# Attention of a diffusion trunk: transposes in three PSUM banks used from both ends, probabilities normalised on GpSimd before them, the sink as a score column

## The chip, the cores and the metric
One core of a Trainium2 chip runs the whole kernel. The metric is the device time of one execution in microseconds, as the median of several runs. The clock that the throttle grants to TensorE is given by the profile as a share of full speed (1.0 is 2.4 GHz, 0.5 is 1.2 GHz).
One core of a Trainium2 chip runs the whole kernel. The metric is the device time of one execution in microseconds, as the median of several runs. The clock that the throttle grants to TensorE is given by the profile as a share of full speed (1.0 is 2.4 GHz, 0.5 is 1.2 GHz).

## What is computed
Two layers of a trunk over 512 latent tokens and 256 context tokens with 1024 features. A layer has a gated feed-forward block (hidden width 2816), a mixer and a second feed-forward block; each starts with an RMS norm with a shift and scale from a conditioning vector. The mixer is the part that matters:

```python
u = modulate(rms_norm(h), shift, scale) @ w_in      # A: 6 query, 2 key, 2 value heads; B: the same; C: 256 channels
A: rotated q, k; each latent query block of 128 reads its own and the two neighbouring key blocks
   (|key - query| <= 128), all 256 context keys and a sink logit:
   p = softmax(concat([q k^T / 8 (masked), q k_ctx^T / 8, sink]))[without the sink]
B: normalised, rotated q, k; each latent query reads all 512 latent and 256 context keys, no sink
C: real part of a 2-D Fourier transform over positions and 64 channels, then a 64x64 map per group
h = h + gate * concat([A, B, C]) @ w_out
```

Context tokens go through the same layer and read only context keys (in A with the sink). In the last layer only the latent tokens' output is needed. Everything is float32.

## The kernel before
The features lie on the 128 partitions, the tokens along the free dimension: `h`, `xh`, `xl` are [128, 8, 768]. A float32 product is made in three passes of a rounded type (fp32r): each factor is split into a high part (`whi`, `xh`, a rounding copy on ScalarE) and a low part (`wlo`, `xl`, the difference, on VectorE), and TensorE adds hi x hi, hi x lo and lo x hi. Weights are streamed: SP loads the tile `raw` (two slots), ScalarE makes `whi` (L602), VectorE makes `wlo` (L938), TensorE multiplies into one of two accumulators `ring` (L1319). Each engine has its own queue in program order; waits are written out by hand as semaphore counts. There is no planner.

The mixer has three parts. First, 12 tiles of `w_in` (`act_w_in`, `dve_w_in`), with head norms and rotation on ScalarE, VectorE and GpSimd; queries and keys go to memory and come back stacked in `k2`, `q2`. After tile j = 1 TensorE makes the combined channel matrix (L1213) from `wf`, a small weight that SP has just loaded, and ScalarE copies it out at j = 2.

Second, the attention. The work is cut into score tiles (branch, key/value head, query block, head of the group), 72 in layer 0 and 48 in layer 1; three consecutive tiles share a query block and are called a trio here. With its context keys a query block has 4 or 5 key blocks of 128 in branch A, 6 in branch B, and 2 if it is a context block (layer 0 only). All engines run the same loop over i, and step i holds different stages of different tiles:

- TensorE: scores of tile i into `ring[i % 2]` (L1242 to L1247); transposes of the probabilities of tile i - LAG into `side` (L1261), a tile of two PSUM banks; and, in three of every three steps, a share of the value products of a finished trio into `bank[0]` (L1280). Before the first share it multiplies a matrix of ones with three diagonal matrices (L1276) into `bank[1]`: that spreads the reciprocal row sums over the partitions.
- VectorE: row maximum of tile i (L887) and a small operation that scales it, and in A takes the larger of it and the sink (L894, L896); the reciprocal of the row sum of tile i - 1 (L910), in A after adding the sink's exponential (L905); the low part `ptl` of the transposed tile i - LAG (L918); for a finished trio the sum of the two output parts (L929) and its product with the spread reciprocals (L931).
- ScalarE: the high part `pth` of the transposed tile (L719), a part of the trio's output (`corr`, L727), the exponential of tile i with its row sum (L737), in A the sink's exponential (L742), and the rounding of the trio's output into `xh` (L750).
- GpSimd: the diagonal matrix ident x reciprocal of each tile, 128 columns (L511), and the output's low part into `xl` (L498).

LAG is 2 and `prob` has P_RING = 3 buffers. The transposes of a tile wait until VectorE has made `ptl` of the tile before:

```python
pe.wait_ge(exp_done, si + 1)
if i >= 1:
    pe.wait_ge(pt_ready, si)
for m in range(nb):
    last = pe.transpose(side[:, m * P:(m + 1) * P], prob[:, i % P_RING, ...], ident[:])
```

At step 2 the loops make the Fourier part (TensorE L1180 and L1193), which uses `side` and both banks. Third, after the loop, 8 tiles of `w_out`: the first waits for the trios' outputs at its later k steps. The split of tile 12 (the first of `w_out`) is made during `w_in`; that of tile 13 (the second) when the first is multiplied. For each output tile VectorE adds the residual (L1044), ScalarE squares it for the next norm (L620), and ScalarE's and VectorE's queues have the split of the next weight tile behind that.

Of the kernel before, what the change touches and what calls it, by code (L numbers as in the profile page):

```python
# [15 lines left out]
F32 = mybir.dt.float32  # L16
# [6 lines left out]
P = 128  # L23
# [22 lines left out]
P_RING, LAG = 3, 2  # L46
# [85 lines left out]

def key_blocks(branch, q):

    if q >= 4:
        return []
    return list(range(max(0, q - 1), min(3, q + 1) + 1)) if branch == 0 else [0, 1, 2, 3]


def build(nc, x_t, ctx_t, c_cols, w_ada, b_ada, gains, g_final, qk_gain, sink, w_in, w_four, w_out,  # L140
# [4 lines left out]
    with ctx:  # L145
# [35 lines left out]
        sinks8 = sb("sinks8", [P, DEPTH * 6])  # L181
# [6 lines left out]
        row_max = sb("row_max", [P, 2])  # L188
        neg_max = sb("neg_max", [P, 4])
        row_sum = sb("row_sum", [P, 4])  # L190
        sink_exp = sb("sink_exp", [P, 4])
        row_tot = sb("row_tot", [P, 2])
# [43 lines left out]
        diag = sb("diag", [P, 2, 3, P], F32, work + 52224)  # L236
# [9 lines left out]
        side = ctx.enter_context(nc.psum_tensor("side", [P, 1024], F32))  # L246
        bank = [ctx.enter_context(nc.psum_tensor(f"bank{i}", [P, 512], F32)) for i in range(2)]
# [7 lines left out]
        cond_ready, sink_ready = sem("cond_ready"), sem("sink_ready")  # L255
# [24 lines left out]
        sc_done, max_done, nm_ready, exp_done = sem("sc_done"), sem("max_done"), sem("nm_ready"), sem("exp_done")  # L280
        tot_done, inv_ready, diag_done = sem("tot_done"), sem("inv_ready"), sem("diag_done")
        sink_exp_done = sem("sink_exp_done")
        p_turned, pth_done, pt_ready, pv_done = sem("p_turned"), sem("pth_done"), sem("pt_ready"), sem("pv_done")
        oadd_done = sem("oadd_done")
# [137 lines left out]
        def _(pool):  # L422
# [49 lines left out]
            for s in stages:  # L472
                layer, n, ow = s["layer"], s["n"], s["out_width"]
                if s["kind"] == "mix":
# [13 lines left out]
                    def rest_out(k):  # L488

                        b, kv, q, g = s["tiles"][3 * k]  # L490
                        tr = s["scores"] // 3 + k
                        here, cols = slice(kv * HD, kv * HD + HD), slice(q * P, (q + 1) * P)
                        pool.wait_ge(ohi_done, tr + 1)

                        pool.wait_ge(diag_done, s["scores"] + min(3 * k + 9, len(s["tiles"])))
                        if k >= 1:
                            pool.wait_ge(olo_done, tr)
                        pool.tensor_tensor(xl[here, 3 * b:3 * b + 3, cols], osum[here, k % 2].rearrange("p (g q) -> p g q", q=P),  # L498
                                           xh[here, 3 * b:3 * b + 3, cols].bitcast(F32), ALU.subtract).then_inc(olo_done, 1)

                    for i, (b, kv, q, g) in enumerate(s["tiles"]):
                        si = s["scores"] + i
                        if i == 0:
                            pool.wait_ge(f1_done, 6 * (layer + 1))
                        if g == 0 and i >= 9:
                            rest_out(i // 3 - 3)
                            pool.wait_ge(olo_done, si // 3 - 2)
# [1054 lines left out]
```

## Time and profile before
| | before |
|---|---|
| runs | 2894.14, 2893.08, 2893.99 us, median 2893.99 |
| profiled execution | 2893.89 us, its span 2892.1 us |
| busy: TensorE, VectorE, ScalarE, GpSimd | 2749.7 (95%), 1503.0 (52%), 1015.9 (35%), 676.7 (23%) us |
| mean granted clock | 0.984 |
| DMA | 274.37 MB |

Layer 0's attention lies between about 752 and 970 us of the span, layer 1's between about 2293 and 2457 us. A row of a view names an operation by its line, its engine and output <- inputs; many tiles share memory, so that `rstd` stands for the trio's output `osum`, `acc` for `corr`, and `v` sometimes for Fourier data. "Idle before" is the time for which the engine stood still ahead of the instruction, with what released it.

### The profile page before, as it was taken

The numbers are of one execution on the slowest core, as the hardware profiler recorded it, in microseconds if no ns is written. First come the engines' busy times: TensorE is split into PE (matmuls) and PEld (weight loads), VectorE is DVE, ScalarE is ACT, GpSimd is POOL, SyncE is SP. The second block draws the span as 40 slices with busy tenths as digits, with TensorE's granted clock in tenths as the row PEclk, the third lists the DMA queues.
The fourth block names the chain that finished last, engine by engine and source line by source line (L and its number), as shares of the span: only waits on it lengthen the run. The fifth ranks groups of instructions, "written<-read, shape, count | busy, mean of one in ns | idle before, by whom it ended". The sixth has DMA issues, their size and how long they took to land.

```text
span 2892.1 us, 37299 instructions
## 1 busy us (share of the span) xinstructions
PE 2749.7 (95%) x15164; PEld 2333.0 (81%) x15164; DVE 1503.0 (52%) x2106; ACT 1015.9 (35%) x1602; POOL 676.7 (23%) x570
## 2 busy tenths in 40 slices
PE   7999999999877899999999999999999887999998
PEld 2888888888666788888888888888887666888887
DVE  2556655644287455575552555754225477533333
ACT  2333333323276343333332333332213266422232
POOL 1233322413033213242321132431011232100001
PEclk8999999999999999999999999999999999999999
DMA  5334333314311123343331233332213420233232
GB/s 218 103 109 134 104 112 111 100 50 161 99 37 27 37 85 109 108 133 106 108 102 58 84 109 123 123 108 64 77 55 107 135 52 1 78 97 102 87 103 79
DMA packets 70586, 274.37 MB, mean 95 GB/s; under 512 B 8720, under 2 KB 12048, under 8 KB 69392
## 3 DMA queue, kind: packets, MB, share of 16 engines
q1 hardware_dynamic: 70416, 271.99, 30.1%
q8 instruction: 120, 1.97, 0.3%
q14 instruction: 50, 0.41, 0.0%
HBM read 258.85 MB, written 13.11 MB: 94 GB/s over the span
## 4 chain that ended last, share of the span: by engine, by line
PE 87%; DVE 7%; ACT 3%; issue 2%; DMA 1%; SPq 1%; POOL 0%; DVEq 0%; ACTq 0%; POOLq 0%
PE ring L1319 72%; PE ring L1328 5%; PE bank L1280 2%; PE side L1261 2%; PE side L1193 1%; PE bank L1426 1%; ACT pth L719 1%; PE bank L1404 1%; DVE wlo L938 1%; PE bank L1276 1%; DVE xl L1037 1%; DVE t L1031 1%; DVE rstd L931 1%; DVE rstd L929 1%; PE ring L1242 1%
## 5 line engine op out<-in xcount | busy, mean ns | idle before, releaser
L1319 PE MATMUL ring<-xh,whi 128*128 128x512 f32 x2760 | 772.7, 348 | 8.6 <-DVE wlo L938 5.0
L1319 PE MATMUL ring<-xh,wlo 128*128 128x512 f32 x2760 | 767.1, 346 | 0.0
L1319 PE MATMUL ring<-xl,whi 128*128 128x512 f32 x2760 | 766.9, 346 | 0.0
L938 DVE TENSOR_TENSOR wlo<-raw,whi 128x1024 fp32r<-128x1024 f32 (+1 forms) x280 | 388.6, 1388 | 512.0 <-ACT whi L602 511.5
L1319 PEld LDWEIGHTS ring<-xh,whi 128*128 128x128 f32 x2760 | 438.4, 189 | 77.4 <-issue 6.3
L1319 PEld LDWEIGHTS ring<-xl,whi 128*128 128x128 f32 x2760 | 438.4, 189 | 68.4
L1319 PEld LDWEIGHTS ring<-xh,wlo 128*128 128x128 f32 x2760 | 437.4, 188 | 68.6
L456 POOL TENSOR_TENSOR ada_acc<-ada_acc,ada_tmp 128x384 f32<-128x384 f32 x252 | 335.2, 1330 | 604.3 <-ACT ada_tmp L614 583.8
L602 ACT ACTIVATE whi<-raw 128x1024 fp32r<-128x1024 f32 (+1 forms) x280 | 314.5, 1123 | 193.2 <-PE ring L1319 182.3
L955 DVE SCALAR_TENSOR_TENSOR ada_acc<-ada_buf,scond,ada_acc 128x384 f32<-128x384 f32 x294 | 353.5, 1202 | 6.9
L1319 PE MATMUL ring<-ah,whi 128*128 128x512 f32 (+1 forms) x1078 | 297.9, 346 | 0.0
L1319 PE MATMUL ring<-al,whi 128*128 128x512 f32 (+1 forms) x1078 | 296.6, 344 | 0.0
L1319 PE MATMUL ring<-ah,wlo 128*128 128x512 f32 (+1 forms) x1078 | 296.5, 344 | 0.0
L778 ACT ACTIVATE ah<-atmp 128x768 fp32r<-128x768 f32 (+1 forms) x88 | 69.8, 793 | 530.0 <-DVE atmp L1103 530.0
L614 ACT ACTIVATE ada_tmp<-ada_buf,scond 128x384 f32<-128x384 f32 x336 | 188.2, 605 | 61.2 <-POOL ada_acc L456 31.0
L1103 DVE TENSOR_TENSOR atmp<-sil,ring 128x768 f32<-128x768 f32 (+1 forms) x88 | 78.1, 888 | 248.6 <-PE ring L1319 246.3
L1044 DVE SCALAR_TENSOR_TENSOR h<-ring,vec_gate,h 128x512 f32<-128x512 f32 x116 | 69.9, 637 | 258.3 <-PE ring L1319 258.2
L773 ACT ACTIVATE sil<-ring 128x768 f32<-128x768 f32 (+1 forms) x88 | 66.7, 758 | 383.5 <-PE ring L1319 383.5
L1319 PEld LDWEIGHTS ring<-ah,wlo 128*128 128x128 f32 x1078 | 170.9, 188 | 25.3
L1319 PEld LDWEIGHTS ring<-al,whi 128*128 128x128 f32 x1078 | 170.8, 188 | 25.3
L1319 PEld LDWEIGHTS ring<-ah,whi 128*128 128x128 f32 x1078 | 170.7, 188 | 24.8
L453 POOL TENSOR_TENSOR ada_acc<-ada_tmp 128x384 f32<-128x384 f32 x42 | 86.6, 2061 | 340.2 <-ACT ada_tmp L614 310.7
(139 smaller groups left out, 2969.3 us busy)
## 6 DMA issues: line engine op xcount, KB each, us to landing
raw<-w_gu SPq DMA_DIRECT2D x176, 512.0 KB, 3.5
ada_buf<-w_ada SPq DMA_DIRECT2D x84, 768.0 KB, 4.2
raw<-w_down SPq DMA_DIRECT2D x64, 704.0 KB, 4.0
raw<-w_in SPq DMA_DIRECT2D x24, 512.0 KB, 3.6
ada_first<-w_ada SPq DMA_DIRECT2D x6, 1536.0 KB, 10.6
raw<-w_out SPq DMA_DIRECT2D x16, 512.0 KB, 3.6
k<-qk_parts SPq DMA_DIRECT2D x16, 384.0 KB, 7.4
q<-qk_parts SPq DMA_DIRECT2D x8, 576.0 KB, 10.0
```

Source lines behind the costliest of these rows:

```text
L453: pool.tensor_tensor(ada_acc[:, 1], ada_tmp[:, 0], ada_tmp[:, 1], ALU.add).then_inc(ada_ctx_done, 2)
L456: pool.tensor_tensor(ada_acc[:, 1], ada_acc[:, 1], ada_tmp[:, k % 2], ALU.add).then_inc(ada_ctx_done, 1)
L602: act.activation(whi[:, slot, 0:nk * P], raw[:, slot, 0:nk * P], ACT.Copy).then_inc(whi_ready, 1)
L614: act.activation(ada_tmp[:, k % 2], ada_buf[:, k], ACT.Copy, scale=scond[:, 1, k:k + 1]).then_inc(ada_prod_done, 1)
L773: act.activation(sil[:, 0:width], ring[0][:, 0:width], ACT.Silu).then_inc(silu_done, 1)
L778: act.activation(ah[:, f, 0:width], atmp[:, 0:width], ACT.Copy).then_inc(ahi_done, 1)
L938: dve.tensor_tensor(wlo[:, slot, 0:nk * P], raw[:, slot, 0:nk * P], whi[:, slot, 0:nk * P].bitcast(F32), ALU.subtract).then_inc(wlo_ready, 1)
L955: dve.scalar_tensor_tensor(out=ada_acc[:, 0], in0=ada_buf[:, k], scalar=scond[:, 0, k:k + 1], in1=ada_acc[:, 0], op0=ALU.mult, op1=ALU.add ...
L1044: last = dve.scalar_tensor_tensor(out=h[:, d, a:b], in0=ring[slot][:, a:b], scalar=vec_gate[:, c, d:d + 1], in1=h[:, d, a:b], op0=ALU.mult ...
L1103: dve.tensor_tensor(atmp[:, 0:width], sil[:, 0:width], ring[1][:, 0:width], ALU.mult).then_inc(prod_done, 1)
L1319: last = pe.matmul(out[:, a:b], w, x[:, k, a:b], start=(i == 0 and m == 0), stop=(i == nk - 1 and m == 2))
L1328: last = pe.matmul(out[:, o:o + b - a], w, x[:, k, a:b], start=(k == 0 and m == 0), stop=(k == nk - 1 and m == 2))
```

## The change
- The PSUM tiles `side` (two banks) and `bank[1]` are now one tile `row` of three banks. Even tiles are transposed into its start, odd ones into its end; with 4 blocks or fewer they don't meet, with 5 one block and with 6 two blocks of each lie in the middle bank. TensorE turns the blocks outside that bank first.
- GpSimd multiplies the whole probability tile by the reciprocal row sums, in place, before it is transposed. The diagonal matrices, the product with ones and L931 are gone.
- GpSimd rounds the trio's output into `xh` (before: ScalarE), in the same place as it makes `xl`.
- The sink is a column of the score tile, put there by a 128x1 product on TensorE; maximum, exponential and row sum take it in. The factor 1/8 goes into the queries (in A in the copy out of `ring`, in B in the norm gain `qkg`), and the maximum is negated by the reduction. The small operations of L894, L896, L905 and the exponential of L742 are gone.
- LAG is 3, P_RING is 4.
- The split of the second `w_out` tile is made at step 5 of the attention.
- The first `w_out` tile's k steps 6, 7, 0, 1 are issued within the attention loop's last steps, then its step 2 and five steps of the second tile, then the last three steps of each.
- The channel matrix is made after tile j = 5 and not after j = 1.

```diff
-P_RING, LAG = 3, 2
+P_RING, LAG = 4, 3
+def turned_from(i, nb):
+    return (i % 2) * (3 * SEQ - nb * P)
-        side = ctx.enter_context(nc.psum_tensor("side", [P, 1024], F32))
-        bank = [ctx.enter_context(nc.psum_tensor(f"bank{i}", [P, 512], F32)) for i in range(2)]
+        row = ctx.enter_context(nc.psum_tensor("row", [P, 1536], F32))
+        side = row[:, 0:1024]
+        bank = [ctx.enter_context(nc.psum_tensor("bank0", [P, 512], F32)), row[:, 1024:1536]]
...
# GpSimd
+                        pool.wait_ge(osum_done, tr + 1)
+                        pool.tensor_copy(xh[here, 3 * b:3 * b + 3, cols], o).then_inc(ohi_done, 1)
...
-                        pool.tensor_scalar(diag[:, i // 3 % 2, g], ident[:], row_inv[:, i % 8:i % 8 + 1], None,
-                                           ALU.mult).then_inc(diag_done, 1)
+                        pool.tensor_scalar(prob[:, i % P_RING, lo:TOK], prob[:, i % P_RING, lo:TOK], row_inv[:, i % 8:i % 8 + 1], None,
+                                           ALU.mult).then_inc(scaled, 1)
...
# ScalarE, w_in
-                if j == 2:
+                if j == 6:
                     act.wait_ge(four_mm, layer + 1)
-                    last = act.activation(un[:, j % 2, 0:width], ring[j % 2][:, 0:width], ACT.Copy)
+                    last = act.activation(un[:, j % 2, 0:width], ring[j % 2][:, 0:width], ACT.Copy, scale=SCALE if j in QA else 1.0)
# ScalarE, attention
+                        if i == 5:
+                            split_hi(t + W_IN_TILES + 1, 1, KD)
...
+                            lo -= b == 0
                             act.activation(prob[:, i % P_RING, lo:TOK], ring[(s["r"] + W_IN_TILES + i) % 2][:, lo:TOK], ACT.Exp,
-                                           bias=neg_max[:, i % 4:i % 4 + 1], scale=SCALE,
+                                           bias=neg_max[:, i % 4:i % 4 + 1],
...
-                            if b == 0:
-                                sc = 6 * layer + 3 * kv + g
-                                act.activation(sink_exp[:, i % 4:i % 4 + 1], sinks[:, sc:sc + 1], ACT.Exp,
...
-                            act.activation(xh[here, 3 * b:3 * b + 3, q * P:(q + 1) * P],
-                                           osum[here, k // 3 % 2].rearrange("p (g q) -> p g q", q=P), ACT.Copy).then_inc(ohi_done, 1)
# VectorE, attention
+                if i == 5:
+                    split_lo(s["t"] + W_IN_TILES + 1, 1, KD)
...
+                    dve.reduce_max(neg_max[:, i % 4:i % 4 + 1], ring[(s["r"] + W_IN_TILES + i) % 2][:, lo:TOK], AX.X,
+                                   negate=True).then_inc(nm_ready, 1)
...
-                    dve.tensor_tensor(o, bank[0][here, 0:3 * P], corr[here, k // 3 % 2], ALU.add).then_inc(oadd_done, 1)
-                    dve.wait_ge(oadd_done, tr + 1)
-                    dve.tensor_tensor(o, o, bank[1][here, 0:3 * P], ALU.mult).then_inc(osum_done, 1)
+                    dve.tensor_tensor(osum[here, k // 3 % 2], bank[0][here, 0:3 * P], corr[here, k // 3 % 2],
+                                      ALU.add).then_inc(osum_done, 1)
# TensorE
-                if j == 1:
+                if j == 5:
                     pe.wait_ge(wf_loaded, 64 * (layer + 1))
...
+                if b == 0:
+                    sc = 6 * layer + 3 * kv + g
+                    pe.matmul(out[:, lo - 1:lo], ident[:], sinks[:, sc:sc + 1], start=True, stop=True)
...
-                pe.wait_ge(exp_done, si + 1)
-                if i >= 1:
-                    pe.wait_ge(pt_ready, si)
+                pe.wait_ge(scaled, si + 1)
+                if i >= 2:
+                    pe.wait_ge(pt_ready, si - 1)
...
+                shared = [m for m in range(nb) if SEQ <= c0 + m * P < 2 * SEQ]
+                for m in [m for m in range(nb) if m not in shared] + shared:
+                    if i >= 1 and shared and m == shared[0]:
+                        pe.wait_ge(pt_ready, si)
+                    last = pe.transpose(row[:, c0 + m * P:c0 + (m + 1) * P], prob[:, i % P_RING, lo + m * P:lo + (m + 1) * P], ident[:])
...
-                    pe.matmul(bank[1][:, 0:3 * P], ones[:], diag[:, k % 2].rearrange("p g q -> p (g q)"), start=True, stop=True)
...
+                if i == len(tiles):
+                    out_part(0, [6])
+                if i == len(tiles) + 1:
+                    out_part(0, [7, 0, 1])
...
+            out_part(0, [2])
+            out_part(1, [6, 7, 0, 1, 2])
+            out_part(0, [3, 4, 5])
+            out_part(1, [3, 4, 5])
```

`out_part(d, ks)` is the product of output tile d over the listed k steps, with the waits that the whole product had.

## Rows read from the trace of the kernel before

**Rows 1.** The page, chain that ended last: share of the span by engine.
```profile
PE 87%; DVE 7%; ACT 3%; issue 2%; DMA 1%; SPq 1%; POOL 0%; DVEq 0%; ACTq 0%; POOLq 0%
```
**Rows 2.** Busy-time window, drain of layer 1: length, PE, PEld, DVE, ACT, POOL, clock, DMA.
```profile
2441.00:2457.00 16.00, 10.18 (x48) 8.63 (x49) 7.33 (x12) 6.57 (x13) 3.38 (x5) 0.89 0.00 1
```
**Rows 3.** TensorE's waits, both attentions (total us, times, longest): layer 0, then 1.
```profile
PE side L1261 <- DVE ptl L918: 23.9, 28, 1.3
PE bank L1276 <- DVE rstd L931: 12.8, 23, 2.3
...
PE side L1261 <- DVE ptl L918: 17.3, 17, 1.3
PE bank L1276 <- DVE rstd L931: 7.7, 15, 3.2
```
**Rows 4.** Chain of waits, attention of layer 1: start, length, what.
```profile
2348.47 0.55 DVE rstd L929
...
2355.72 0.55 DVE rstd L929
...
2363.80 0.57 DVE rstd L929
...
2397.62 0.55 DVE rstd L929
...
2398.19 0.56 DVE rstd L931
...
2398.88 0.88 PE bank L1276 x2
...
2406.41 0.55 DVE rstd L929
```
**Rows 5.** Timeline of TensorE, one tile's six transposes: start, length.
```profile
2442.20 0.84 PE L1261 MATMUL side<-ident,prob 128*128 128x128 f32 x6 [1.29 <-DVE ptl L918]
```
**Rows 6.** Groups by shape, 785 to 960 and 960 to 1060 us: busy us, mean ns.
```profile
L918 DVE TENSOR_TENSOR ptl<-side,pth 128x768 fp32r<-128x768 f32 x24 | 22.8, 951 | 14.0 <-ACT pth L719 14.0
L887 DVE TENSOR_REDUCE row_max<-ring 128x1 f32<-128x768 f32 x24 | 22.8, 950 | 2.6 <-PE ring L1247 2.3
L737 ACT ACTIVATE prob<-ring,neg_max 128x768 f32<-128x768 f32 x24 | 21.7, 902 | 4.8 <-DVE neg_max L896 4.5
L719 ACT ACTIVATE pth<-side 128x768 fp32r<-128x768 f32 x24 | 19.5, 812 | 16.6 <-PE side L1261 16.5
...
L1382 PE MATMUL side<-ones,acc 128*128 128x1 f32 x12 | 2.1, 242 | 0.2 <-ACT sq L620 0.2
```
**Rows 7.** Groups by shape, GpSimd, whole span.
```profile
L511 POOL TENSOR_SCALAR diag<-ident,row_inv 128x128 f32<-128x128 f32 x120 | 72.7, 606 | 305.2 <-DVE row_inv L910 235.7 <-PE bank L1180 69.2
L469 POOL TENSOR_TENSOR acc<-acc,sq 128x768 f32<-128x768 f32 x25 | 46.2, 1849 | 181.6 <-ACT sq L620 181.2 <-POOL acc L466 0.2
L498 POOL TENSOR_TENSOR xl<-rstd,xh 64x384 fp32r<-64x384 f32 x40 | 40.4, 1010 | 21.6 <-ACT xh L750 16.6
...
L466 POOL COPY acc<-sq 128x768 f32<-128x768 f32 x5 | 4.1, 828 | 158.2 <-ACT sq L620 150.2 <-issue 8.0
```
**Rows 8.** Timelines of VectorE, then ScalarE, at the first output tiles of layer 0.
```profile
979.27 1.14 DVE L1044 SCALAR_TENSOR_TENSOR h<-ring,vec_gate,h 128x512 f32<-128x512 f32 x2 [3.24 <-PE ring L1319]
982.28 1.23 DVE L938 TENSOR_TENSOR wlo<-raw,whi 128x1024 fp32r<-128x1024 f32 x1 [1.87 <-ACT whi L602]
987.60 1.14 DVE L1044 SCALAR_TENSOR_TENSOR h<-ring,vec_gate,h 128x512 f32<-128x512 f32 x2 [4.09 <-PE ring L1319]
...
980.45 0.85 ACT L620 ACTIVATE sq<-h 128x768 f32<-128x768 f32 x1 [5.74 <-DVE h L1044]
981.20 1.05 ACT L602 ACTIVATE whi<-raw 128x1024 fp32r<-128x1024 f32 x1
```
**Rows 9.** TensorE's waits at the start of the mixers: layer 0, then layer 1.
```profile
PE bank L1213 <- DMA wf<-w_four: 0.9, 1, 0.9
...
PE bank L1213 <- DMA wf<-w_four: 1.4, 1, 1.4
```

More of the change, by code:

```diff
@@ L235, in build @@
         prob = sb("prob", [P, P_RING, TOK], F32, work + 43008)
-        diag = sb("diag", [P, 2, 3, P], F32, work + 52224)
         pth = sb("pth", [P, 2, 6, 3 * P], F32R, work + 55296)
@@ L688, in _ @@
             act.wait_ge(more_loaded, 16 * 5)
-            act.activation(sinks8[:], sinks[:], ACT.Copy, scale=1.0 / SCALE).then_inc(sink_ready, 1)
+            for l in range(DEPTH):
+                last = act.activation(qkg[:, 2 * l:2 * l + 1], qkg[:, 2 * l:2 * l + 1], ACT.Copy, scale=SCALE)
+            last.then_inc(qkg_ready, 1)
             split_hi(0, 0, NK[0])
@@ L718, in _ @@
                                 act.wait_ge(pv_done, tr - 1)
+                            c0 = turned_from(j, nb)
                             act.activation(pth[:, j // 3 % 2, 0:nb, g * P:(g + 1) * P],
-                                           side[:, 0:nb * P].rearrange("p (n q) -> p n q", q=P), ACT.Copy).then_inc(pth_done, 1)
+                                           row[:, c0:c0 + nb * P].rearrange("p (n q) -> p n q", q=P), ACT.Copy).then_inc(pth_done, 1)
                         k = i - LAG - 5
@@ L874, in dve_fourier, with dve_attention @@
                 dve.tensor_tensor(xl[:, 6 + c, 0:wd], side[:, 0:wd], xh[:, 6 + c, 0:wd].bitcast(F32), ALU.subtract).then_inc(flo_done, 1)
-        def dve_attention(dve, s):
+        def dve_attention(dve, s, split_lo):
             layer, tiles = s["layer"], s["tiles"]
-            sinks_before = len(tiles) // 2 and sum(len(score_tiles(l)) // 2 for l in range(layer))
             for i in range(len(tiles) + LAG + 6):
@@ L915, in dve_attention @@
                     nb = len(key_blocks(b, q)) + 2
+                    c0 = turned_from(j, nb)
                     dve.wait_ge(pth_done, sj + 1)
                     part = slice(g * P, (g + 1) * P)
-                    dve.tensor_tensor(ptl[:, j // 3 % 2, 0:nb, part], side[:, 0:nb * P].rearrange("p (n q) -> p n q", q=P),
+                    dve.tensor_tensor(ptl[:, j // 3 % 2, 0:nb, part], row[:, c0:c0 + nb * P].rearrange("p (n q) -> p n q", q=P),
                                       pth[:, j // 3 % 2, 0:nb, part].bitcast(F32), ALU.subtract).then_inc(pt_ready, 1)
@@ L1271, in weigh_values @@
                     pe.wait_ge(v_ready, 4 * (layer + 1))
-                    pe.wait_ge(diag_done, s["scores"] + 3 * k + 3)
                     if k >= 1:
                         pe.wait_ge(osum_done, tr)
-                    pe.matmul(bank[1][:, 0:3 * P], ones[:], diag[:, k % 2].rearrange("p g q -> p (g q)"), start=True, stop=True)
-                    return
-                for m in range(len(keys) * (part - 1) // 3, len(keys) * part // 3):
+                for m in range(len(keys) * part // 4, len(keys) * (part + 1) // 4):
                     for pt in (pth, ptl):
@@ L1283, in weigh_values, with out_part @@
                     last.then_inc(pv_done, 1)
+            ready = dict(zip((0, 3), out_counts(layer)))
+            ready[6] = 2 * layer + 2
+            def out_part(d, ks):
+                rr = r + len(tiles) + d
+                if ks[0] == 6:
+                    slot_free(pe, rr)
+                    pe.wait_ge(wlo_ready, t + d + 1)
+                for k in ks:
+                    if k in ready:
+                        pe.wait_ge(flo_done if k == 6 else olo_done, ready[k])
+                    w_h, w_l = whi[:, d, k * P:(k + 1) * P], wlo[:, d, k * P:(k + 1) * P]
+                    for m, (w, x) in enumerate(((w_h, xh), (w_h, xl), (w_l, xh))):
+                        for lo, hi in spans(s["out_width"]):
+                            last = pe.matmul(ring[rr % 2][:, lo:hi], w, x[:, k, lo:hi], start=(k == 6 and m == 0), stop=(k == 5 and m == 2))
+                if ks[-1] == 5:
+                    last.then_inc(mm_done, 1)
             for i in range(len(tiles) + LAG + 3):
```

82 lines of the change are left out of this document (23 added, 59 removed).

## The prediction

> **What bounds the kernel now.** First the page's chain of waits: the reader sees that almost the whole end-setting chain is TensorE in the plain products, which the change leaves alone [rows 1]. So only stretches in which TensorE stands still can pay. The busy-time windows find them in the two attention stages, and most plainly at the end of the second: TensorE is busy 10.18 of 16 us at a mean granted clock of 0.89 [rows 2]. TensorE's own waits say what it waits for: 23.9 us (layer 0) and 17.3 us (layer 1) for the low part ptl of the tile before, because there is one tile `side` to turn into, and 12.8 and 7.7 us for the second operation on the output (L931), because the normalising sum is made in the same bank as before; the longest of those, 2.3 and 3.2 us, lie in the drain [rows 3]. That is 61.7 us in all, the pool from which this change must live, and some removed TensorE work.
>
> The chain, read inside the attention, gives the period. A trio is three score tiles that share a query block; the start of L929 (one per trio) marks it. With 4 key blocks a trio takes 2355.72 - 2348.47 = 7.25 us, with 5 it takes 2363.80 - 2355.72 = 8.08, with 6 it takes 2406.41 - 2397.62 = 8.79 [rows 4]. In the last, three turns go round a ring of dependences: six transposes 0.84 us, ACT's pth 0.81, VectorE's ptl 0.95 and hand-offs of some 0.2 make 2.8 us a tile, 8.4 a trio [rows 5, 6]. VectorE's own work is near it: 3 x (0.95 + 0.95) + 0.55 + 0.56 = 6.8 us and the small operations.
>
> **The change part by part.**
> *Turning into three banks, L931 and the diagonal product gone.* In the chain of the six-block trio L931 (0.56 us) and the product ones x diag (0.88 us for two passes as the chain counts it) stand one behind the other [rows 4]; both go, which leaves 8.79 - 1.44 = 7.35. The next one late is the ring, now shorter: with 6 blocks only the middle bank is shared, so two transposes of six (taken as 0.4 us) instead of six stand between ptl of one tile and pth of the next: 0.4 + 0.81 + 0.95 + 0.2 = 2.4 a tile; in the tile in which VectorE also has the one output addition it is VectorE's 0.95 + 0.95 + 0.55 + about 0.2 of small operations = 2.65. That makes 2.4 + 2.4 + 2.65 = 7.45. The two ways agree within 0.1; I take 7.5, a gain of 1.3 a trio. For 4 blocks, where nothing is shared and the ring falls to half, and for 5, the 1.44 leaves the chain as well and VectorE loses two of four small operations besides; the sink column's TensorE product comes in, at most 0.24 us by the 128x1 row and less where its load overlaps the product before it [rows 6], so up to 0.7 a trio of the windowed half, on an engine that waits some 45 us in 24 trios, 1 to 2 us in each [rows 3]. I take 1.2 for them, and for the two-block trios. After the first trio layer 0 has 23 intervals, 8 of them with six blocks, layer 1 has 15, 8 of them with six: 16 x 1.3 + 22 x 1.2 = 47 us. Bounds of one trio: nothing gained, and 8.79 less VectorE's remaining 3 x 1.9 + 0.55 = 6.25, that is 2.5; half of that is what I take.
>
> *GpSimd scales the whole probability tile.* The trace has only its product on 128 columns: 606 ns [rows 7]. On 768 columns it needs at least what a copy of that size takes, 0.83 us; the copy costs at most 1.08 ns a column, so the 640 further columns cost 0.69 if this form streams like a copy: 1.3 us. At the slope of a two-input operation, (1849 - 1010)/384 = 2.18 ns a column, it would be 606 + 1395 = 2.0 us. If the 606 are nearly all per column, as four and more ns a column, it would be 606 x 6 = 3.6 us at the very worst and 2.75 with the 0.18 us fixed that the two-input rows leave (1849 - 768 x 2.18). I take 1.3, by the nearest row with one tensor input. A trio then costs GpSimd 3 x 1.3, the output's difference 1.01 and the new rounding copy, at most 0.6: 5.5 us of 7.5, and it is hidden. It stays hidden up to 1.95 us a tile. What it holds up: the turn of the tile waits for it, and behind that turn on TensorE the rest of the value products and the next scores; one more tile of lag and a fourth probability buffer cover one period, 2.5 us, for reciprocal and scaling.
> The Trainium skill speaks against this part: "GPSIMD Engine Reference", section 7, gives four cycles an element for a loop with a dependent fp32 chain, and section 3.1 about one cycle for a body of one or two operations. As an estimate from that page and 1.2 GHz, the six-block tile would cost 2.6 us by the first and about 1.1 us by the second, so the sum would come out on the losing side or as forecast; the 606 ns row alone cannot tell the two apart, and the first is the first rival below. The same page says that GpSimd shares its ports with VectorE operations that have two SBUF inputs. ptl is 951 ns with a PSUM input [rows 6], and of the operations of the attention only the early split of a weight has two SBUF inputs.
>
> *ScalarE* loses the sink exponential and the output's rounding; the scale moves into the queries and costs an immediate. It has 3 x (0.90 + 0.81) of 7.5 us in the six-block trio [rows 6]: covered before and after, 0.
>
> *Longer pipeline and the early split.* One more tile of lag costs a period with little in it at each start, about 1.2 us. The split of the second output weight comes in at i = 5: 1.05 on ScalarE, 1.23 on VectorE [rows 8], of which VectorE shows all: 1.2. Per layer 2.4, together 5 us. SP's order of transfers is not touched; the split lets raw's next load start earlier, which nobody waits for.
>
> *The output product drawn forward.* In the drain TensorE idles 5.8 of 16 us in layer 1 [rows 2]; four of eight k steps of the first output tile go there, 4.2 us in layer 0, where two residuals start 987.60 - 979.27 = 8.33 us apart for eight steps [rows 8], and two thirds of it, 2.7, in layer 1, whose output is 512 columns wide and not 768; the first five steps of tile 1 cover the last output split, where before the product started at once. With less idle time the clock of 0.89 should come back to near 1: 16 x 0.1 = 1.5 us a layer. Against it: tile 1 then has only three k steps left behind tile 0's end (3.1 and 2.1 us), while the weight of tile 2 needs residual 1.14, square 0.85, split 1.05 and 1.23, one behind the other, 4.3 us and hand-offs [rows 8]. Before, all of it lay beside a whole tile. So a new wait of about 1.4 us in layer 0 and (with narrower operations) 1.6 in layer 1. Net: 4.2 + 2.7 + 3 - 3 = 7, of which I take 6.
>
> *Channel product at j = 5.* TensorE waited 0.9 and 1.4 us for wf [rows 9]; by j = 5 it has long landed. What is late next are the splits of w_in and, in layer 1, the stacked queries; their chains start behind the same place and move with it. 2 us. The two tiny scalings of qkg at the start replace one: 0.
>
> Sum: 47 - 5 + 6 + 2 = 50 us. From the profiled execution's 2893.89 us (span 2892.1 and 1.8 around it; 0.1 from the median of 2893.99) that is 2844.
>
> **The rivals.**
> *GpSimd becomes the bound* (the one on the other side). For it: 606 ns for 128 columns is 4.7 ns a column, when a copy has 1.08. Against: a fixed share is unknown. With 0.18 + 3.34 ns a column, 2.75 us at 768, 2.3 at 640, 1.9 at 512, 1.0 at 256, a trio costs GpSimd three of these and about 2 us of output work and hand-offs: 10.2, 9.0, 7.6 and 5.1 us. Against 8.79, 8.08, 7.25 and about 6: 16 x 1.4 + 8 x 0.9 + 6 x 0.4 - 8 x 0.9 = 25 lost, 5 for the start, 8 back for drain and wf: 2916. The change turns slower from about 2.25 us a six-block tile.
> *GpSimd at two-input pace*, 2.0 us: 8.0 a six-block trio, 7.2, 6.3 and 4.7 for the others; gain 16 x 0.8 + 8 x 0.9 + 14 x 1.0 = 34, with the other terms 37: 2857.
> *The wait only changes its name.* TensorE must reach the shared bank's wait after scores, value products and four transposes in the same in-order queue; if order and not the ring sets the tile, as the 8.79 against the ring's 8.4 hints, only half comes out: 23 - 5 + 6 + 2 = 26: 2868.
> *The new wait in the output product eats the drain* (no prefetch long enough, clock not back): 6 less, 2850; it lies in the forecast's own range.
>
> **How the numbers follow.** Forecast 0.57, GpSimd at two-input pace 0.12, wait renamed 0.13, GpSimd the bound 0.18. The forecast's own range is 2826 (1.9 a trio) to 2856; the two middle cases take it to 2868, and some of the slow one's milder forms to 2890, where about one in ten is left above. Low end 2826, one in ten below at most. Faster by over 0.2% (5.8 us, about what a measurement tells from no change): 0.80; slower 0.17; between 0.03, for a scaling close to 2.25 us.
>
> **What would show it.** Right: GpSimd's product on 128x768 near 1.3 us; six-block trios (one output addition each) 7.5 us apart; TensorE's wait for ptl under 15 us in both layers together and none for a second output operation; no wait for wf; a new wait of 1 to 2 us before output tile 2. Wrong: the scaling above 2 us and TensorE's turn waiting for GpSimd; six-block trios over 8.3; VectorE's ptl or maximum longer than 0.95 us because GpSimd is busy beside them.

## The result, and the profile after

The changed kernel takes 2855.43 us (median of 4 runs, 2851.39 to 2859.47) against 2894.06 (2893.08 to 2897.23) for the kernel before on the same chip: ratio 0.9863, 95% interval 0.985 to 0.9877, 38.6 us less. The forecast was 2844, with 2826 to 2890 around it. The profiled executions have spans of 2892.1 and 2855.7 us; their difference of 36.4 us is what the stages below add up to.

The page's chain that ended last, changed kernel (share of the span by engine, then by line). GpSimd had 0% of it before [rows 1], and VectorE 7%:

```profile
PE 85%; POOL 6%; DVE 4%; issue 2%; ACT 2%; DMA 1%; SPq 0%; POOLq 0%; DVEq 0%; ACTq 0%
PE ring L1324 72%; PE ring L1333 6%; POOL prob L509 5%; PE row L1172 1%; DVE wlo L917 1%; PE bank L1261 1%; POOL xl L499 1%; PE ring L1281 1%; PE row L1431 1%; ACT whi L600 1%; DVE t L1010 1%; DVE xl L1016 1%; PE row L1246 1%; PE bank L1409 0%; PE row L1409 0%
```

The groups by shape of GpSimd over the whole span, changed kernel (busy us, mean ns of one, idle time before them and its releaser). They answer to [rows 7]:

```profile
L509 POOL TENSOR_SCALAR prob<-prob,row_inv 128x768 f32<-128x768 f32 x48 | 105.2, 2202 | 2.2 <-DVE row_inv L890 0.6
L509 POOL TENSOR_SCALAR prob<-prob,row_inv 128x640 f32<-128x640 f32 x24 | 45.0, 1883 | 10.4 <-DVE row_inv L890 10.0
L499 POOL TENSOR_TENSOR xl<-rstd,xh 64x384 fp32r<-64x384 f32 x40 | 40.2, 1005 | 3.4
L509 POOL TENSOR_SCALAR prob<-prob,row_inv 128x512 f32<-128x512 f32 x24 | 37.4, 1564 | 108.3 <-DVE row_inv L890 107.6
L509 POOL TENSOR_SCALAR prob<-prob,row_inv 128x256 f32<-128x256 f32 x24 | 22.1, 922 | 9.5 <-DVE row_inv L890 9.1
L495 POOL CAST xh<-rstd 64x384 fp32r<-64x384 f32 x40 | 20.0, 500 | 11.1 <-DVE rstd L909 8.7
```

The reader sees two things. The scaling of a six-block tile takes 2.20 us, not 1.3. And its 48 instructions have 2.2 us of idle time in front of them all together: in the six-block tiles GpSimd hardly ever waits, so it is the engine that sets the pace. The chain of waits in the six-block stretch of layer 0 says so directly (start, length, what):

```profile
859.84 0.50 POOL xh L495
...
860.43 1.02 POOL xl L499
...
861.54 2.15 POOL prob L509
...
863.72 4.38 POOL prob L509 x2
...
868.17 0.50 POOL xh L495
```

From one rounding to the next are 868.17 - 859.84 = 8.33 us, and only GpSimd is in it: 3 x 2.18 + 0.50 + 1.02 leaves 0.27 for five hand-offs. Before, a six-block trio took 8.79 and its chain ran over VectorE and TensorE [rows 4].

TensorE's waits in the attention of layer 0, changed kernel (total us, times, longest); of [rows 3], the line for ptl has shrunk from 23.9 to 2.2, and the second operation on the output is gone:

```profile
PE row L1246 <- POOL prob L509: 14.5, 19, 1.9
PE bank L1261 <- DVE rstd L909: 12.1, 12, 2.1
...
PE row L1246 <- DVE ptl L899: 2.2, 2, 1.8
PE ring L1324 <- DVE wlo L917: 1.3, 1, 1.3
```

In layer 1 the same lines read 10.4, 6.2, 2.2 and, for the weight of the output, 1.8. The wait at the bank has kept its size (12.8 and 7.7 before) and changed its releaser, from the second operation on the output to the first.

VectorE's groups by shape, layer 0, changed kernel: 957 and 949 ns where [rows 6] has 951 and 950. A GpSimd that is busy without a pause beside them did not slow them:

```profile
L899 DVE TENSOR_TENSOR ptl<-row,pth 128x768 fp32r<-128x768 f32 x24 | 23.0, 957 | 20.8 <-ACT pth L722 20.5
L882 DVE TENSOR_REDUCE neg_max<-ring 128x1 f32<-128x768 f32 x24 | 22.8, 949 | 0.7 <-PE ring L1229 0.6
```

The ledger of the two spans, from the starts of marking instructions (the clearing of `wf` for a mixer's start, the output addition for the trios, the third residual for the output):

```
stage                                  layer 0                layer 1
w_in and first Fourier half        119.63 -> 115.94       109.73 -> 101.99
second Fourier half                 12.45 ->  10.75         8.55 ->   8.55
to the first output addition        16.38 ->  17.95        15.08 ->  18.90
from it to the last one            170.79 -> 156.37       124.32 -> 112.01
to the third residual of w_out      25.29 ->  22.07        16.75 ->  17.79
```

So the trios gave 26.7 us (forecast 47), the longer start cost 5.4 (forecast 5), w_in gave 11.4 (forecast 2), drain and output 2.2 (forecast 6). These are differences of one execution each; a second execution of the changed kernel (the last run below) moves single terms by up to 2.6 us. What lies outside the two mixers moved by some 0.2 us in the other direction. The 1.7 us of the second Fourier half is left out of the account: every other version has 10.75 there, the one with only the channel matrix moved included, so it belongs to the one execution of before.

### The profile page after: what moved, and what is told of

It is laid out like the page before. It is cut to its first block, busy times and chain, and to the rows that moved or that the text cites. A ratio compares the mean times of both kernels' runs of the same rounds, so it can differ in the third digit from the quotient of the medians.

```text
span 2855.7 us, 37039 instructions
## 1 busy us (share of the span) xinstructions
PE 2733.2 (96%) x15204; PEld 2329.7 (82%) x15204; DVE 1450.7 (51%) x1886; ACT 980.9 (34%) x1503; POOL 833.2 (29%) x610
## 4 chain that ended last, share of the span: by engine, by line
PE 85%; POOL 6%; DVE 4%; issue 2%; ACT 2%; DMA 1%; SPq 0%; POOLq 0%; DVEq 0%; ACTq 0%
PE ring L1324 72%; PE ring L1333 6%; POOL prob L509 5%; PE row L1172 1%; DVE wlo L917 1%; PE bank L1261 1%; POOL xl L499 1%; PE ring L1281 1%; PE row L1431 1%; ACT whi L600 1%; DVE t L1010 1%; DVE xl L1016 1%; PE row L1246 1%; PE bank L1409 0%; PE row L1409 0%
## 5 line engine op out<-in xcount | busy, mean ns | idle before, releaser
L1324 PE MATMUL ring<-xh,whi 128*128 128x512 f32 (+1 forms) x2712 | 753.5, 346 | 10.6 <-DVE wlo L917 7.0
L1324 PE MATMUL ring<-xl,whi 128*128 128x512 f32 (+1 forms) x2712 | 750.5, 345 | 0.0
L1324 PE MATMUL ring<-xh,wlo 128*128 128x512 f32 (+1 forms) x2712 | 750.0, 345 | 0.0
L1324 PEld LDWEIGHTS ring<-xh,whi 128*128 128x128 f32 x2712 | 428.2, 188 | 76.8 <-issue 8.6
L1324 PEld LDWEIGHTS ring<-xh,wlo 128*128 128x128 f32 x2712 | 429.0, 188 | 66.5
L1324 PEld LDWEIGHTS ring<-xl,whi 128*128 128x128 f32 x2712 | 428.4, 188 | 64.9
L509 POOL TENSOR_SCALAR prob<-prob,row_inv 128x768 f32<-128x768 f32 (+3 forms) x120 | 209.4, 1755 | 130.4 <-DVE row_inv L890 127.3
```

The source lines that it names most:

```text
L509: pool.tensor_scalar(prob[:, i % P_RING, lo:TOK], prob[:, i % P_RING, lo:TOK], row_inv[:, i % 8:i % 8 + 1], None, ALU.mult).then_inc(scale ...
L1324: last = pe.matmul(out[:, a:b], w, x[:, k, a:b], start=(i == 0 and m == 0), stop=(i == nk - 1 and m == 2))
```

## The experiments

Each ran in three timed rounds beside the kernel before (medians 2894.94, 2895.52 and 2895.25 us in the three groups). "Changed" is the changed kernel.

### The channel matrix alone

```diff
 kernel before:
-                if j == 1:                       # TensorE: channel matrix
+                if j == 5:
-                if j == 2:                       # ScalarE: its copy
+                if j == 6:
```

> The kernel before with one edit: the channel matrix is made after tile j = 5 (and copied out at j = 6) instead of j = 1 and 2. Theory (the product's place is worth what the stage took less in the changed kernel: the clock falls behind the wait for wf and every later chain of the stage starts later): 8 to 11 us faster, about 3.5 of it in layer 0's w_in part and 5 or more in layer 1's. Rival (my forecast's term: only the waits for wf of 0.9 and 1.4 us go): 2 to 3 us faster, and the rest of what w_in gained in the changed kernel has another cause.

Measured: 2884.42 us (2881.19 to 2889.21), ratio 0.9967 (0.9954 to 0.998). The stage w_in takes 116.53 and 104.43 us, 3.1 and 5.3 less than before, out of a wait of 0.9 and 1.4 [rows 9]. The windows of busy time show most of the rest (length, PE, PEld, DVE, ACT, POOL, clock, DMA): the first 30 us from the start of mixer 1, then the whole stage in layer 0 and in layer 1. The kernel before:

```profile
2199.00:2209.00 10.00, 8.60 (x65) 8.21 (x64) 2.41 (x5) 5.52 (x9) 0.32 (x1) 0.92 0.39 113
2209.00:2219.00 10.00, 9.89 (x48) 8.21 (x47) 3.58 (x6) 1.20 (x2) 3.52 (x3) 0.91 0.13 41
2219.00:2229.00 10.00, 6.87 (x36) 5.64 (x35) 5.95 (x9) 3.95 (x8) 4.34 (x3) 0.94 0.34 116
...
651.37:771.00 119.63, 115.63 (x658) 97.80 (x657) 47.22 (x72) 37.46 (x59) 31.87 (x26) 0.99 0.52 157
2199.76:2309.49 109.73, 97.86 (x472) 78.86 (x470) 49.48 (x72) 33.92 (x59) 27.73 (x20) 0.94 0.49 149
```

The same stretches with the channel matrix alone moved, where mixer 1 starts at 2191.45:

```profile
2191.00:2201.00 10.00, 10.00 (x73) 9.31 (x73) 2.94 (x5) 5.94 (x8) 0.32 (x1) 1.00 0.39 113
2201.00:2211.00 10.00, 8.52 (x44) 6.88 (x43) 5.37 (x11) 2.92 (x5) 3.80 (x3) 1.00 0.19 52
2211.00:2221.00 10.00, 8.19 (x51) 7.26 (x50) 5.56 (x9) 2.71 (x5) 4.07 (x2) 1.00 0.78 295
...
651.62:768.15 116.53, 113.83 (x666) 96.93 (x664) 47.18 (x72) 37.45 (x59) 31.83 (x26) 1.00 0.54 161
2191.45:2295.88 104.43, 94.28 (x472) 76.35 (x470) 49.27 (x72) 33.93 (x59) 29.26 (x20) 0.97 0.52 157
```

Without the wait at j = 1 the granted clock of these 30 us is 1.00 where it was 0.91 to 0.94, and in the kernel before it stays low for 30 us more (0.88, 0.97 and 0.86). Priced as TensorE busy throughout, which makes it an upper bound, the whole stage's clock costs 0.06 x 109.7 = 6.6 us before and 0.03 x 104.4 = 3.1 after the move in layer 1, 1.2 and nothing in layer 0. With the two waits that is up to 7.0 of the 8.4 us.

### The change without it

```diff
 changed kernel:
-                if j == 5:  ...  if j == 6:
+                if j == 1:  ...  if j == 2:
```

> The changed kernel with the channel matrix back after j = 1 (copied out at j = 2). Theory: 8 to 11 us slower than the changed kernel (2863 to 2867). Rival: 2 to 3 us slower.

Measured: 2865.25 us (2861.79 to 2869.04), ratio 0.99 (0.9885 to 0.9914). That is some 10 us above the changed kernel, with w_in at 119.37 and 109.18 us. The move is worth about 10 us in both directions, alone and within the change. The clock of the stage comes and goes with it: 0.99 and 0.94 here, 1.00 and 0.98 in the changed kernel. Of the 5.3 us that the channel matrix alone gave in layer 1, the wait is 1.4 and the clock at most 3.5. Also seen, and in part the same time, is this: the copies out of `ring` for tiles 1 and 2 stand 15.36 us apart before and 11.21 in the changed kernel (16.31 and 12.75 in layer 0). How much of that is order and how much clock was not separated, nor which of TensorE's short waits the clock answers to.

### GpSimd scales at most 384 columns

```diff
 changed kernel:
+                        hi = min(lo + 3 * P, TOK)
-                        pool.tensor_scalar(prob[:, i % P_RING, lo:TOK], prob[:, i % P_RING, lo:TOK], ...
+                        pool.tensor_scalar(prob[:, i % P_RING, lo:hi], prob[:, i % P_RING, lo:hi], ...
```

> The changed kernel, but GpSimd scales only the first 384 columns of a probability tile (the rest stays unscaled: that part of the normalisation is left out). By 0.28 + 2.5 ns a column such an operation takes 1.24 us, about the 1.3 us that my forecast gave the whole tile. Theory (GpSimd's pace sets the trio: 3 x 2.20 + 0.50 + 1.01 and hand-offs = 8.33): six-block trios fall from 8.33 to 7.5 us, five-block ones by about 0.5, and the time by 15 to 22 us, to some 2835. Rival (TensorE's in-order queue with the shared bank holds the trio at about 8.3 whatever GpSimd does): under 4 us.

This kernel leaves out a part of the normalisation: what lies behind the first 384 columns of a tile stays unscaled. Measured: 2840.0 us (2838.05 to 2843.55), ratio 0.9813 (0.9799 to 0.9828). The output additions on VectorE's timeline, six-block trios of this kernel:

```profile
862.20 0.56 DVE L910 TENSOR_TENSOR rstd<-bank,acc 64x384 f32<-64x384 f32 x1
869.74 0.54 DVE L910 TENSOR_TENSOR rstd<-bank,acc 64x384 f32<-64x384 f32 x1
877.22 0.54 DVE L910 TENSOR_TENSOR rstd<-bank,acc 64x384 f32<-64x384 f32 x1
```

Distances of 7.54 and 7.48 us, and the intervals of both layers come to 143.2 + 105.0, that is 46.9 us less than before. These are the numbers of the forecast, 7.5 and 47. TensorE no longer waits for GpSimd. So the account of what is late next was right, and GpSimd's time alone kept the changed kernel from it.

### One place to turn into

```diff
 changed kernel:
-    return (i % 2) * (3 * SEQ - nb * P)
+    return 0
-                if i >= 2:
-                    pe.wait_ge(pt_ready, si - 1)
+                if i >= 1:
+                    pe.wait_ge(pt_ready, si)
```

> The changed kernel, but all tiles are transposed into the start of the three banks and each waits for ptl of the tile before, as in the kernel before. Theory (GpSimd sets the six-block trio at 8.33, the ring of dependences in one place needs 3 x 2.8 = 8.4): the six-block trios stay within 0.4 us of 8.33, the four- and five-block ones lose up to 0.5, in all 2 to 10 us slower. Rival (the two ends carry the gain): back to 8.8 a trio and 20 us or more slower.

Measured: 2866.5 us (2860.74 to 2868.1), ratio 0.9901 (0.9884 to 0.9917). The chain of waits in a six-block trio of this kernel:

```profile
866.59 0.89 PE row L1246 x6
...
867.50 0.82 ACT pth L722
...
868.34 0.97 DVE ptl L899
...
869.45 0.86 PE row L1246 x6
```

That is the ring that was inferred before, now bare: six transposes 0.87, pth 0.82, ptl 0.97 and hand-offs of 0.17 make 2.83 a tile and 8.49 a trio, and no longer the 8.79 of [rows 4]. By time this kernel is 11 us slower than the changed one, just above the expected 2 to 10. The intervals give 21.1 us of the changed kernel's 26.7. So, with GpSimd as slow as it is, the three banks bring only 5.6 us of the intervals, and where the rest of the 11 lies was not followed up; the 21.1 come from what this kernel shares with the changed one, the removed second output operation, diagonal products and small operations and the longer lag, which were not taken apart.

### Both of these

```diff
 changed kernel: the scaling of at most 384 columns, and one place to turn into
```

> The short scaling (only 384 columns of a tile, the rest of the normalisation left out) together with the transposes in one place, each waiting for ptl of the tile before. With GpSimd out of the way this shows what the three banks are worth. Theory (the ring transposes, pth, ptl and hand-offs of 2.8 us a tile binds again): six-block trios 8.4 to 8.6 against 7.5 with both ends, 18 us or more slower than the short scaling alone. Rival (the earlier 8.5 was GpSimd's pace and not the ring): 7.5 to 7.8 and under 6 us slower.

This kernel too leaves the scaling of the further columns out. Measured: 2863.54 us (2861.1 to 2867.55), ratio 0.9895 (0.988 to 0.9911). Six-block trios 8.49 us. Against one place with the full scaling this is the same within the runs' spread: with one place the ring (8.49) is late and hides GpSimd (8.33). Against the short scaling in three banks it is 23.5 us slower. The two bounds, 8.49 for the ring of one place and 8.33 for GpSimd, stand almost on top of each other; either cure alone brings almost nothing in the six-block trios, both together bring 1 us in each.

### The rounding of the output back on ScalarE

```diff
 changed kernel:
-                        pool.tensor_copy(xh[here, 3 * b:3 * b + 3, cols], o).then_inc(ohi_done, 1)      # GpSimd
+                            act.activation(xh[here, ...], osum[here, ...], ACT.Copy).then_inc(ohi_done, 1)   # ScalarE, k = i - LAG - 6, as before
```

> The changed kernel, but the rounding of a trio's output into xh is ScalarE's again, as before the change. Theory (GpSimd sets the trio, so its 0.50 us and a hand-off come straight off): six-block trios 8.33 -> 7.75, five-block ones 0.3 less, 8 to 12 us faster than the changed kernel. Rival (ScalarE's queue, with exponential and pth in it, is as tight and takes the 0.52 us on): less than 3 us either way.

Measured: 2843.38 us (2841.21 to 2848.43), ratio 0.9825 (0.9806 to 0.9845). Six-block trios 7.76 us: 8.33 less the 0.50 of the rounding and a hand-off of 0.07. The chain there is still GpSimd's. ScalarE took the work at no visible cost.

### LAG 2 with four probability buffers

```diff
 changed kernel:
-P_RING, LAG = 4, 3
+P_RING, LAG = 4, 2
```

> The changed kernel with LAG 2 instead of 3 (P_RING stays 4). Theory (exponential, reciprocal and 2.2 us of scaling do not fit between a tile's exponential and its turn two steps later, so every tile waits for GpSimd with its latency and not only its throughput): six-block trios 9 us or more, 15 us or more slower than the changed kernel. Rival (GpSimd's throughput of 8.33 a trio is the bound with either lag, and a shorter lag saves the start): within 4 us, or faster by up to 3.

Measured: 2924.77 us (2921.54 to 2930.94), ratio 1.0108 (1.009 to 1.0127), the only version slower than before. The chain of waits in the six-block stretch of this kernel:

```profile
890.06 2.21 POOL prob L509
...
892.34 0.50 POOL xh L495
...
892.92 1.02 POOL xl L499
...
894.03 4.38 POOL prob L509 x2
898.41 2.02 issue
...
900.49 2.20 POOL prob L509
```

GpSimd does the same 8.3 us of work, and then stands still for some 2 us in each trio: 900.49 - 890.06 = 10.43. Its timeline says that it waits for VectorE's reciprocal:

```profile
900.49 2.20 POOL L509 TENSOR_SCALAR prob<-prob,row_inv 128x768 f32<-128x768 f32 x1 [2.07 <-DVE row_inv L890]
```

That reciprocal follows an exponential (898.55) which ScalarE's queue has behind pth of an earlier tile (897.20), and that pth behind a turn (896.29) which waited for GpSimd. With a lag of two tiles, scaling, turn, exponential and reciprocal stand in one loop. TensorE's waits in the attention of layer 0 of this kernel name it:

```profile
PE row L1246 <- POOL prob L509: 49.0, 47, 2.1
```

### The output tiles in their old order

```diff
 changed kernel:
-                if i == len(tiles):       out_part(0, [6])
-                if i == len(tiles) + 1:   out_part(0, [7, 0, 1])
-            out_part(0, [2]); out_part(1, [6, 7, 0, 1, 2]); out_part(0, [3, 4, 5]); out_part(1, [3, 4, 5])
+            out_part(0, [6, 7, 0, 1, 2, 3, 4, 5]); out_part(1, [6, 7, 0, 1, 2, 3, 4, 5])
```

> The changed kernel, but output tiles 0 and 1 are made one after the other behind the attention loop, none of their steps drawn forward. Theory (drawing forward fills the drain, but shortens the cover of tile 2's weight split): the wait ahead of output tile 2 (1.3 and 1.8 us) is gone, the drain idles 4.2 and 2.7 us more with a lower clock after it; net 3 to 7 us slower. Rival (my ledger of the two profiles, which shows only 2 us gained from the last output addition to the third residual): within 2 us of the changed kernel.

Measured: 2858.77 us (2857.46 to 2859.79), ratio 0.9876 (0.9859 to 0.9893). By the medians 3 us slower than the changed kernel, inside the spread of both; by the ledger, trios and output together, 179.42 against 178.44 in layer 0 and 128.53 against 129.80 in layer 1, nothing. So it lies between nothing and 3 us, and the expected 3 to 7 were not shown.

### Tile 1 holds more back

```diff
 changed kernel:
-            out_part(1, [6, 7, 0, 1, 2])
+            out_part(1, [6, 7, 0])
             out_part(0, [3, 4, 5])
-            out_part(1, [3, 4, 5])
+            out_part(1, [1, 2, 3, 4, 5])
```

> The changed kernel with one order changed: output tile 1 has its steps 6, 7, 0 ahead of tile 0's last three and 1 to 5 behind them (before: five ahead, three behind). Theory (tile 2's weight split, 4.3 us and hand-offs behind tile 0's end, needs five steps of tile 1 as cover): the wait ahead of output tile 2 falls from 1.3 us to 0 in layer 0 and from 1.8 to under 1 in layer 1, where the clock stays up; 2 to 5 us faster. Rival (the last trio's output becomes late instead, as only 4 steps cover it): 0.

Measured: 2854.29 us (2850.76 to 2857.28), ratio 0.9861 (0.9838 to 0.9883); not told apart from the changed kernel by time. In the ledger the output of layer 0 is 1.4 us shorter, trios and output of layer 1 together 2.8. What this order takes away is the new wait: none is left before output tile 2 in layer 0, and 0.5 us of 1.8 in layer 1. In the changed kernel, TensorE's timeline in front of output tile 2 of layer 1 (start, length, what, idle time before and its releaser) reads:

```profile
2428.02 0.39 PE L1281 MATMUL ring<-xh,wlo 128*128 128x512 f32 x1
2430.24 0.47 PE L1324 MATMUL ring<-xh,whi 128*128 128x512 f32 x1 [1.84 <-DVE wlo L917]
...
2431.60 0.63 PE L1324 MATMUL ring<-xh,wlo 128*128 128x512 f32 x1
2432.03 0.63 PE L1324 MATMUL ring<-xh,whi 128*128 128x512 f32 x1
...
2434.59 0.47 PE L1324 MATMUL ring<-xh,whi 128*128 128x512 f32 x1
```

After the 1.84 us of standing still the first products run at nearly full pace; from 2431.60 on they start 0.43 us apart for 3 us, twice the 0.23 of their full pace: 7 of them, 1.4 us on top of the wait. The window of these 3 us has the granted clock at half (length, PE, PEld, DVE, ACT, POOL, clock, DMA):

```profile
2431.60:2434.60 3.00, 3.00 (x9) 2.35 (x8) 1.46 (x1) 0.77 (x1) 1.19 (x1) 0.50 0.36 143
```

It does not always come. The changed kernel run again has the same wait of 1.84 us, and behind it a clock of 1.00 and the full pace:

```profile
2430.20 0.47 PE L1324 MATMUL ring<-xh,whi 128*128 128x512 f32 x1 [1.84 <-DVE wlo L917]
...
2431.66 0.40 PE L1324 MATMUL ring<-xh,whi 128*128 128x512 f32 x1
2431.89 0.39 PE L1324 MATMUL ring<-xl,whi 128*128 128x512 f32 x1
```

Nine profiled executions have this order of output tiles 0 and 1, and all nine have the wait of 1.84 us. In six the clock then falls to half for some 3 us, and the second and third residual are 7.6 us apart; in three it stays at 1.00, and they are 6.0 apart. What decides between the two was not found.

### Both late cures together

```diff
 changed kernel: the rounding on ScalarE, and tile 1 holding more back
```

> The changed kernel with both: rounding on ScalarE, and tile 1's steps 3 ahead and 5 behind. Theory: the two gains add, 10 to 16 us faster than the changed kernel, some 2841, because they lie in different stretches. Rival: as for the single edits, under 5 us.

Measured: 2842.97 us (2839.95 to 2845.87), ratio 0.9821 (0.9803 to 0.984). It is the best complete version, 12 us below the changed kernel, nearly all of it from the rounding; the second part adds nothing that the times can show.

### The sink apart from the scores

```diff
 changed kernel:
-                    pe.matmul(out[:, lo - 1:lo], ident[:], sinks[:, sc:sc + 1], start=True, stop=True)
+    ScalarE:  sink_exp = exp(sink - max);  VectorE:  max(row_max, sink), row_sum + sink_exp   (as before, in A)
```

> The changed kernel, but the sink is handled as before: no score column, its exponential on ScalarE, the larger of it and the maximum and its addition to the row sum as two more small VectorE operations in each tile of the windowed half (60 tiles). Theory (GpSimd sets most windowed trios too, so VectorE's 0.3 us a tile more lie beside it): under 4 us slower than the changed kernel. Rival (the two-block and four-block trios are VectorE's or the hand-offs' and carry it): 6 to 12 us slower.

Measured: 2868.66 us (2866.88 to 2870.43), ratio 0.9912 (0.9897 to 0.9927), 11.4 us above the changed kernel of the same group. By the two profiled executions, whose spans differ by 14.5, only 0.2 us of this are in the attention (16.91 + 157.07 in layer 0, 19.08 + 114.45 in layer 1, against 19.39 + 154.73 and 18.83 + 114.35); against the first execution of the changed kernel it is 2.3. The rest lies where no instruction differs: 3.6 us up to the first mixer, 7.8 between the mixers and 3.0 in the two stages of w_in. In the window from 72 to 640 us, this kernel:

```profile
72.00:640.00 568.00, 566.58 (x3274) 494.33 (x3273) 322.34 (x360) 183.86 (x258) 171.98 (x120) 1.00 0.33 104
```

and the changed kernel run again beside it:

```profile
72.00:640.00 568.00, 565.21 (x3283) 495.94 (x3281) 325.74 (x363) 185.51 (x260) 172.24 (x120) 1.00 0.33 104
```

Same clock, TensorE busy throughout, and nine products fewer in the same time. Some records of products can be missing from a trace, but the stage's length says the same. The cause stays open; it was not tried further. The number 11 is the rival's, but its reason, slower trios, is not seen: the sink column itself is worth 2 us at most in the attention.

### The changed kernel again

> The changed kernel as it is, to have it on the same chip as the three others. Both theories: 0.985 to 0.988 of the kernel before, six-block trios 8.33 us.

Measured: 2857.27 us (2849.3 to 2858.69), ratio 0.9866 (0.9844 to 0.9889); six-block trios 8.33 us as the first time. Its ledger shows how far single terms can be trusted: against the kernel before, the trios give 26.0 us here (26.7 the first time), the longer start costs 6.8 (5.4), w_in gives 12.4 (11.4), drain and output 4.7 (2.2). Of that last difference 1.6 us are the stretch behind the new wait, at half clock the first time and not here.

## Why the prediction was right, and where not

The direction and the range held, and the time missed by 11 us. It holds in part by luck, because two errors of opposite sign met: the trios gave 20 us less than forecast, and w_in 9 more. The changed kernel with the channel matrix back at j = 1, which takes the second error out, runs in 2865.25 us, outside the forecast's own range of 2826 to 2856. And of the signs that the prediction had named for being wrong, two of three came: a scaling above 2 us with TensorE's turn waiting for GpSimd, and six-block trios over 8.3 (8.33). The third, the slower VectorE beside a busy GpSimd, did not.

*What bounds the kernel, and the pool to live from*: right in the place. The whole difference lies in the two mixers, though 11 us of it come from w_in, which the pool of 61.7 us did not count.

*The next one late is the ring, 7.5 us a six-block trio, 47 us in all*: right under its own condition, shown by the short scaling (7.5 us, 46.9 us). Of the two ways to the 7.5, the one by the chain was wrong in its parts: taking away the 1.44 of the second operation and the diagonal product alone gave 0.3 in a six-block trio (8.49 with one place), since the ring stood right behind. What shortens the ring is the three banks: with GpSimd out of the way, one place has 8.49 us and three banks 7.5.

*GpSimd scales 768 columns in 1.3 us and is hidden behind the 7.5*: this is the step that failed. It takes 2.20 us and sets the six-block trio at 8.33. 922, 1564, 1883 and 2202 ns at 256, 512, 640 and 768 columns are 0.28 us and 2.50 ns a column. At 128 columns this gives 0.60, the 606 ns of [rows 7]; one size could not tell the fixed part from the slope. The value lies between the two bounds that were worked out (2.0 and 2.75), above the 1.95 up to which it was said to be hidden and below the 2.25 from which it costs. The prediction took the nearest row in kind, a copy, and not the pace of a two-input operation. The Trainium skill gives in "GPSIMD Engine Reference", section 7, four cycles an element for a dependent fp32 chain, and in section 3.1 about one for a body of one or two operations. At that page's 1.2 GHz the measured 2.50 ns are 3.0 cycles, so neither is the pace of this operation, the first is the nearer, and the measured rows decide.

What came true is the rival "GpSimd at two-input pace": 8.0 us a trio and 2857, where 8.33 and 2855.43 were measured. The forecast gave it 0.12. GpSimd was the bound, but at a price below the old one, so the rival on the other side did not come. Its break-even of 2.25 us a tile was set too low: at 2.20 the kernel is still 38.6 us faster, and 0.05 more in each of the 48 six-block tiles would take back only 2.4.

*The wait only changes its name*: partly so, for TensorE now waits 24.9 us for GpSimd instead of 41.2 for ptl. But TensorE's order of work does not hold the tile at 8.3, since the short scaling reaches 7.5.

*Longer start and early split, 5 us*: 5.4 and 6.8 measured. *LAG 3* is needed: with 2 the GpSimd loop costs 67 us.

*Output drawn forward, 6 us*: mis-sized. 2.2 and 4.7 measured by the ledgers of two executions, and nothing to 3 when it is undone. The new wait was foreseen with its size (1.4 and 1.6; 1.3 and 1.84 measured), but not the stretch at half clock that followed it in layer 1 in six of nine executions.

*Channel matrix, 2 us*: mis-sized, and about 10. The forecast counted the wait alone. Behind it stood the clock (over the stage 0.99 and 0.94 against 1.00 and 0.97, at most 4.7 us). With the waits of 2.3 that leaves 1.4 or more of the 8.4, for which a longer way from tile 1 to tile 2 is the likely cause, which was not shown.

*The low end, 2826 (1.9 a trio)*: this does not come out of the prediction's own sum. With 1.9 in all 38 intervals it gives 2819, with 1.9 in the 16 six-block ones alone 2834.

The sum with measured terms: 26.7 - 5.4 + 11.4 + 2.2 + 1.7 - 0.2 = 36.4.

## What to carry to other kernels

Before work is moved to an engine, its time must be read at two sizes; one size leaves the slope open by a factor of four, and where the threshold (1.95 us) lies between the bounds, the chance belongs to both sides. When one loop's bound is lifted, work out the bound of every other loop beside it: 8.49 and 8.33 us looked like one, and only both cures together gave the microsecond. A wait of TensorE can cost more than its length: 1.4 us more behind 1.84, when the granted clock fell to half after it, in six of nine executions, and nothing more in the other three; in a sum it deserves a range of its own, and one profile does not give it.

## What was not expected of the hardware

A scaling on GpSimd with one tensor input and a scalar per partition (0.28 us and 2.50 ns a column) is slower per column than its sum or difference of two tensors (2.18 ns, from 1849 and 1010 ns in [rows 7]), and 2.3 times slower than its copy (at most 1.08).

A program with 180 small operations more in the attention (two on VectorE and one on ScalarE in each of 60 tiles) ran 11 us slower, mainly in stretches of plain products that it shares with the other, at clock 1.00 in both. Why was not found. A change of 10 us between two versions is therefore not yet proof for the place at which they differ; the ledger by stages has to agree.
